# MoBA's position bias: from two TensorE products per head to VectorE, and the two heads' value products interleaved

## The reference, cut to what matters

```
s_own = einsum('bhqd,bhkd->bhqk', q_c, k_own) + rel_bias[:, rel_bucket(q_pos - k_pos)]
s_own = where(k_pos <= q_pos, s_own, -inf)
probs = softmax(s_own)
out   = einsum('bhqk,bhkd->bhqd', probs, v_own)
```

## Time and profile before

| | |
|---|---|
| median of the runs | 2476.46 us (2475.26 to 2477.57) |
| span of the profiled execution | 2475.7 us |
| PE busy | 2411.7 us, 97% |
| PEld busy | 2055.0 us, 83% |
| DVE busy | 1606.0 us, 65% |
| ACT busy | 1033.3 us, 42% |
| mean granted TensorE clock | 0.994 |
| MoBA stage of layer 0 | 302.98 to 327.60 us |
| MoBA stage of layer 1 | 1001.31 to 1025.93 us |

### The profile page before, as it was taken

The page is one execution under the profiler, slowest core; times in us unless marked ns, Lnnn a source line. Parts: engine busy times, 40 slices in busy tenths (PEclk is TensorE's granted clock), DMA queues, the critical chain, the costliest instruction groups (busy, mean ns, idle before and its releaser), DMA issues. The chain is left out here.

```text
span 2475.7 us, 41693 instructions
## 1 busy us (share of the span) xinstructions
PE 2411.7 (97%) x17447; PEld 2055.0 (83%) x17447; DVE 1606.0 (65%) x2242; ACT 1033.3 (42%) x1365; POOL 99.2 (4%) x179
## 2 busy tenths in 40 slices
PE   7999999999999999999999999999999999998999
PEld 7999989999999999899999854464888887647999
DVE  6887756778888887657798632671744442474555
ACT  5445534454554455335454321661422222263333
POOL 2010000001101100000001000000000000000000
PEclk9999999999999999999999999999999999999999
DMA  8776503647777775116467742102532331212452
GB/s 283 251 271 216 168 3 120 205 145 267 252 254 239 272 244 160 46 54 213 162 229 255 272 155 68 52 2 71 167 102 90 98 102 52 81 56 69 162 195 69
DMA packets 270807, 381.97 MB, mean 154 GB/s; under 512 B 9593, under 2 KB 235209, under 8 KB 268994
## 3 DMA queue, kind: packets, MB, share of 16 engines
q1 hardware_dynamic: 251628, 314.47, 38.7%
q0 software_dynamic: 18128, 64.20, 7.2%
q10 hardware_dynamic: 902, 1.15, 0.2%
HBM read 366.13 MB, written 13.65 MB: 153 GB/s over the span
## 5 line engine op out<-in xcount | busy, mean ns | idle before, releaser
L704 PE MATMUL ps<-span 128*128 128x512 f32 x1280 | 453.9, 399 | 2.3 <-issue 1.2
L635 PE MATMUL ps<-span,w_low 128*128 128x256 f32 x1440 | 408.0, 283 | 0.0
L706 PE MATMUL ps<-span,w_low 128*128 128x256 f32 x1280 | 359.5, 281 | 0.0
L633 PE MATMUL ps<-span 128*128 128x256 f32 x1216 | 348.6, 287 | 8.2 <-DVE span L1585 5.2
L1603 DVE TENSOR_TENSOR w_low<-ring,span 128x2048 fp32r<-128x2048 f32 x131 | 299.8, 2288 | 82.3 <-ACT span L1267 82.3
L1267 ACT ACTIVATE span<-ring 128x2048 fp32r<-128x2048 f32 x131 | 250.6, 1915 | 135.5 <-DMA ring<-in_ffn_w_in 112.8
L704 PEld LDWEIGHTS ps<-span 128*128 128x128 f32 x1280 | 240.6, 188 | 60.3 <-issue 1.3
L635 PEld LDWEIGHTS ps<-span,w_low 128*128 128x128 f32 x1440 | 277.0, 192 | 0.0
L634 PE MATMUL ps<-span 128*128 128x256 f32 x864 | 245.3, 284 | 0.0
L633 PEld LDWEIGHTS ps<-span 128*128 128x128 f32 x1216 | 233.8, 192 | 12.4 <-DVE w_low L1603 5.4
L706 PEld LDWEIGHTS ps<-span,w_low 128*128 128x128 f32 x1280 | 241.9, 189 | 0.0
(11 more groups left out here) (487 smaller groups left out, 5337.3 us busy)
## 6 DMA issues: line engine op xcount, KB each, us to landing
ring<-in_ffn_w_in SPq DMA_DIRECT2D x88, 1024.0 KB, 8.9
ring<-in_w_mlp SPq DMA_DIRECT2D x64, 1024.0 KB, 5.3
wmod<-in_w_mod POOLq DMA_DIRECT2D x96, 512.0 KB, 6.8
ring<-in_ffn_w_out SPq DMA_DIRECT2D x44, 1024.0 KB, 5.2
ring<-in_w_mix_in SPq DMA_DIRECT2D x26, 1024.0 KB, 5.5
ring<-in_xattn_w_kv SPq DMA_DIRECT2D x16, 1024.0 KB, 5.4
mod_scratch<-mod_acc POOLq DMA_DIRECT2D x24, 512.0 KB, 6.2
ring<-mod_scratch SPq DMA_DIRECT2D x12, 1024.0 KB, 4.9
```

Of the source, the lines that this page charges most:

```text
L633: mm(dst, w_hi, x_hi, start=start, stop=False, **more)
L635: return mm(dst, w_lo, x_hi, start=False, stop=stop, **more)
L704: mm(ps[bank + m].rearrange("p (w t) -> p w t", w=2), hi[:, k, cols], span[:, :, k, :], start=(k == 0), stop=False, skip_group_check=True)
L706: last = mm(ps[bank + m][:, 0:T], lo[:, k, cols], h_high[:, k, :], start=False, stop=(k == KD - 1), skip_group_check=True)
```

## The change: the bias is added by VectorE, and a pair's value products alternate

The table becomes `toep`, with toep[p, h, t] = bias_rows[h, 127 - p + t], so that its rows stand in the order of the queries and nothing has to be reversed. To read it with one DMA of positive strides, GpSimd first stores 128 copies of each row (2 MB where it was 16 KB) and reads with a row stride of 511. The reversing matrix leaves the constants.

TensorE's `scores(h)` keeps the two products of queries and keys alone. For h >= 4 it waits for the two maxima of head h - 4, no longer for the exponentials. VectorE's two row maxima become two `tensor_tensor_reduce`: each adds scores from PSUM and bias from `toep`, writes the sum to `prob` and the row maximum to `smx`. For h >= 4 it waits first for the turn of head h - 4, the last reader of that slot of `prob`. ScalarE takes the exponential in place, from `prob` to `prob`, and the wait for the turn leaves it. The wait for the table moves from TensorE to VectorE.

`out(h)` becomes `out_pair(pair)`: the products of the even and the odd head over the first 128 keys, then the two over the last 128 keys, one after the other. It waits for both heads' `probT`. It stands at even steps h >= 4, between scores(h) and turn(h - 2), and the last pair comes at the end.

```diff
             def scores(h):
                 if h >= 4:
-                    pe.wait_ge(*sm_act.at(l, 2 * (h - 3)))
+                    pe.wait_ge(*sm_max.at(l, 3 * (h - 4) + 2))
-                mm(bank[:, 0:T], cst["flip"], hank[:, h, :], start=True, stop=False,
-                mm(bank[:, T:T + P], cst["flip"], hank[:, h, P:T], start=False, stop=False,
...
+                mm(bank[:, 0:T], mq[hi, pair, P:T], mk[hi, pair, :], start=True, stop=True)
+                mm(bank[:, T:T + P], mq[hi, pair, 0:P], mk[hi, pair, 0:P], start=True, stop=True
+                   ).then_inc(*sc_done.up())
...
+            def out_pair(pair):
+                pe.wait_ge(*pt_ready.at(l, 2 * pair + 2))
+                if pair >= 2:
+                    pe.wait_ge(*av_out.at(l, pair - 1))
+                bank = ps[6 + pair % 2]
+                for k, at, width in ((0, 0, T), (1, P, P)):
+                    for e in range(2):
+                        h = 2 * pair + e
+                        last = mm(bank[e * HD:(e + 1) * HD, at:T], mv[:, k, h * HD:(h + 1) * HD],
+                                  probT[:, e, k * T:k * T + width], start=(k == 0), stop=(k == 1),
+                                  skip_group_check=True)
+                        if k == 1:
+                            last.then_inc(*av_done.up())
...
-            for h in range(NH + 3):
+            for h in range(NH + 2):
                 if h < NH:
                     scores(h)
+                if h >= 4 and h % 2 == 0:
+                    out_pair((h - 4) // 2)
                 if 2 <= h < NH + 2:
                     turn(h - 2)
-                if h >= 3:
-                    out(h - 3)
+            out_pair(NPAIR - 1)
...
-                pool.dma_start(scratch["bias"], bias_rows).then_inc(bias_stored.sem, 16)
+                pool.dma_start(scratch["bias"], bias_rows.rearrange("h (o t) -> h o t", o=1).to_broadcast(
+                    [NH, P, 2 * T])).then_inc(bias_stored.sem, 16)
                 pool.wait_ge(bias_stored.sem, 16)
                 src = scratch["bias"]
-                pool.dma_start(hank[:, :, :], bass.AP(src.tensor, 0, [[1, P], [2 * T, NH], [1, T]])
+                pool.dma_start(toep[:, :, :], bass.AP(src.tensor, P - 1, [[2 * T - 1, P], [P * 2 * T, NH], [1, T]])
                                ).then_inc(bias_stored.sem, 16)
...
             def exponential(h):
-                e, g, bank = h % 4, base + h, ps[banks[h % 4]]
+                e, g = h % 4, base + h
+                bank = prob[:, e, :] if biased else ps[banks[h % 4]]
                 act.wait_ge(*sm_max.at(l, 3 * (g + 1)))
-                if h >= 4:
-                    act.wait_ge(*pt_done.at(l, g - 3))
...
             def maxima(h):
                 e, g = h % 4, base + h
                 dve.wait_ge(*sc_done.at(l, g + 1))
+                if biases and h >= 4:
+                    dve.wait_ge(*pt_done.at(l, g - 3))
...
+                    if biases:
+                        v.tensor_tensor_reduce(prob[:, e, at:at + w], ps[banks[e]][:, at:at + w], biases(h, t), 1.0,
+                                               -3.0e38, ALU.add, ALU.max, smx[:, e, t:t + 1]).then_inc(*sm_max.up())
+                    else:
+                        v.tensor_reduce(smx[:, e, t:t + 1], ps[banks[e]][:, at:at + w], AX_X, ALU.max
+                                        ).then_inc(*sm_max.up())
...
+            if l == 0:
+                dve.wait_ge(bias_stored.sem, 32)
+            maxima, weights = softmax(l, 0, 1.0, (T, P), SCORE_BANKS, lambda h, t: toep[:, h, t * P:T])
```

More of the change, by code:

```diff
@@ L113, in constants @@
         "head_ones": f(r // HD == c // HD),
-        "flip": f(r + c == P - 1),
         "eye": f(j == t),
@@ L270, in program @@
         store["v_loaded"] = [Signal(ctx, nc, f"v_loaded{s}") for s in range(RING2)]
-        scratch = {"bias": nc.dram_tensor("bias_scratch", (NH, 2 * T), F32).ap(),
+        scratch = {"bias": nc.dram_tensor("bias_scratch", (NH, P, 2 * T), F32).ap(),
                    "mod": nc.dram_tensor("mod_scratch", (DEPTH, P, 2, MODS * P), F32).ap()}
@@ L312, in build_first @@
         part("under_mem", [P, KD, T])
-        part("under_hank", [P, NH, T])
+        part("under_toep", [P, NH, T])
         g_low = part("g_low", [P, KD, T])
@@ L335, in build_first @@
     mem_sb = sb("mem_sb", [P, KD, T])
-    hank = sb("hank", [P, NH, T])
+    toep = sb("toep", [P, NH, T])
     mix_buf = sb("mix_buf", [P, RAW + 4 * T])
@@ L789, in scores @@
                 if h >= 4:
-                    pe.wait_ge(*sm_act.at(l, 2 * (h - 3)))
+                    pe.wait_ge(*sm_max.at(l, 3 * (h - 4) + 2))
                 hi = slice(hb, hb + HD)
-                mm(bank[:, 0:T], cst["flip"], hank[:, h, :], start=True, stop=False,
-                   skip_group_check=True)
-                mm(bank[:, T:T + P], cst["flip"], hank[:, h, P:T], start=False, stop=False,
[L796 to L800, removed]
+                mm(bank[:, 0:T], mq[hi, pair, P:T], mk[hi, pair, :], start=True, stop=True)
+                mm(bank[:, T:T + P], mq[hi, pair, 0:P], mk[hi, pair, 0:P], start=True, stop=True
+                   ).then_inc(*sc_done.up())
             def turn(h):
@@ L809, in turn @@
                 last.then_inc(*pt_done.up())
[L811 to L814, removed]
+            def out_pair(pair):
+                pe.wait_ge(*pt_ready.at(l, 2 * pair + 2))
+                if pair >= 2:
                     pe.wait_ge(*av_out.at(l, pair - 1))
[L816 to L820, removed]
+                bank = ps[6 + pair % 2]
[7 more added lines that the diff above has]
+                            last.then_inc(*av_done.up())
             pe.wait_ge(*mix_evac.at(l, MIX_TILES - 1))
-            if l == 0:
-                pe.wait_ge(bias_stored.sem, 32)
-            for h in range(NH + 3):
+            for h in range(NH + 2):
                 if h < NH:
                     scores(h)
+                if h >= 4 and h % 2 == 0:
+                    out_pair((h - 4) // 2)
                 if 2 <= h < NH + 2:
                     turn(h - 2)
-                if h >= 3:
-                    out(h - 3)
+            out_pair(NPAIR - 1)
         def heads_of(e):
@@ L1340, in cross_part, with softmax @@
                ).then_inc(*cross_high.up())
-        def softmax(l, base, scale, widths, banks):
+        def softmax(l, base, scale, widths, banks, biased=False):
             def exponential(h):
-                e, g, bank = h % 4, base + h, ps[banks[h % 4]]
+                e, g = h % 4, base + h
+                bank = prob[:, e, :] if biased else ps[banks[h % 4]]
                 act.wait_ge(*sm_max.at(l, 3 * (g + 1)))
-                if h >= 4:
-                    act.wait_ge(*pt_done.at(l, g - 3))
                 at = 0
@@ L1469, in scalar_program @@
             col_high(l, KV0)
-            exponential, turned = softmax(l, 0, 1.0, (T, P), SCORE_BANKS)
+            exponential, turned = softmax(l, 0, 1.0, (T, P), SCORE_BANKS, True)
             for h in range(NH + 2):
@@ L1751, in shift, with softmax @@
                                                b[:, m, 1:T + 1], ALU.mult, ALU.add), mixed)
-        def softmax(l, base, scale, widths, banks):
+        def softmax(l, base, scale, widths, banks, biases=None):
             def maxima(h):
@@ L1969, in vector_program @@
             step(l, v.memset(state[:, :, :], 0.0), seq_step)
-            maxima, weights = softmax(l, 0, 1.0, (T, P), SCORE_BANKS)
+            if l == 0:
+                dve.wait_ge(bias_stored.sem, 32)
+            maxima, weights = softmax(l, 0, 1.0, (T, P), SCORE_BANKS, lambda h, t: toep[:, h, t * P:T])
             evac = moba_out(l)
```

2 lines of the change are left out of this document (removed).

## The result

The changed kernel is slower: 2497.18 us median of 4 runs (2493.37 to 2503.82), beside 2477.02 of the kernel before on the same chip (2475.26 to 2479.95). The ratio is 1.0088, with an interval of 1.007 to 1.0105. The forecast was 2471.1 us, the range up to 2477.5. Its profiled execution took 2495.78 us with a span of 2493.8, against a span of 2475.7 before: 18.1 us more.

The account below looks back on a forecast made before the run. TensorE's issue was taken to bound the stage before, a cross-engine loop and VectorE after. Gaining 2.7 us in each of two layers, 5.4, takes 2475.7 to 2470.3; plus 0.8 gives 2471.1 us, range 2467 to 2477.5.

Parts of the forecast that it names:

- The edits that I cost at nothing: Table store of 2 MB: some 12 us, up to twice that under load, weight loads still in time; no cost.
- The walk: Layer 0's stage laid out by durations and engine orders: solver starts at 325.56, a gain of 2.67 us.
- anywhere outside the two stages: Sign against the forecast: time moving outside this stage of layer 0 and its twin in layer 1.
- The loop: Stage, across TensorE, VectorE and ScalarE: out_pair waits for ScalarE's copy; 3.95 + M, 4.8 us a pair against 5.96.
- TensorE's terms: TensorE's work per pair in the stage: scores 2 x 0.85, turns 2 x 0.48, value products 0.80, together 3.46 us.
- The stage at full clock: Layer 0's stage after the change, from 302.98 to some 325.1; 22.10 us forecast.
- M: VectorE's time for both row maxima of a head with the new instruction: 0.85 us, between 0.62 and 0.93.
- The first (TensorE stays the limit, 2456.5): Rival in the stage: TensorE stays the limit, gain 10.0 us a layer, 2456.5 us; chance 0.07.
- The second (a slow instruction): Rival on VectorE: new instruction slow, slower from M = 1.26; 2479.9 us at M = 1.50; chance of slower 0.12.
- The third (no overlap of alternated products): Rival on TensorE: alternated products don't overlap with 256 columns, 1.60 us a pair; 2475.8 us, no change; chance 0.04.

Follow-up runs that it names:

- e2: The kernel before with the 2 MB store alone, 128 copies of each row from SBUF; 2493.18 us, ratio 1.0067.
- e10: The kernel before with 16 KB stored once, then copied 128-fold from DRAM to DRAM, heads as outer dimension; 2474.48 us, ratio 0.9995.
- e5: e1 with unread TensorE products filling every gap: 4 behind the scores of head 2, then 2, 3, 4, 1 before the pairs; 2472.96 us.
- e3: e1 with four unread TensorE products behind the scores of head 2; 2478.33 us, ratio 1.0006.
- e8: e1 with ScalarE's copy before the exponential, VectorE's low half at step 9, unread products behind head 2's scores and before pairs 3 and 4; 2466.98 us.
- e11: e8 with only the 3 unread products behind the scores of head 2, none before the pairs; 2462.76 us, ratio 0.995.
- e1: The changed kernel with the 16 KB store again, rows reversed in the table and read backwards by VectorE; 2483.01 us, ratio 1.0026.
- e4: The kernel before with the alternated value products (out_pair) alone, flip products and small store kept; 2482.23 us, ratio 1.0017.
- e9: The kernel before with 16 KB stored once, then copied 128-fold from DRAM to DRAM, copies as outer dimension; 2475.06 us, ratio 0.999.

## Why the prediction was wrong

**The step that failed first** is "The edits that I cost at nothing". It took the 2 MB store from the rate of a load to 128 partitions, 1 MB in 6.0 us, at 12 us and "at up to twice that under load". It took 45.0, with the ring's loads at 37.0, where a delay of "as much as 10 us" was allowed for. The step looked for who waits for the table, and there it was right: the table landed 45 us before VectorE asked for it. What counted were the ring's loads, under way on another queue at the same time. e2 shows this alone at 12.57 us of late start; e10 shows that the source, not the bytes, made it so. The price was in no row of before, and the text bounded it by a row of another kind of source.

**The second failed step** is "The walk". The stage of before stood "at full clock", and the walk took every duration of the new one at that clock, with no term for its loss. The text itself put 1.1 us of idle time ahead of each out_pair, and its walk leaves TensorE with nothing between the third head's scores, done by 302.98 + 3 x 0.85 = 305.53, and the first turn (maxima 2, behind the weights that this turn needs, stand at 306.75). It never asked what a TensorE that is busy 1.5 of 4 us does to its clock. In before the flip products filled this time beside their own job; unread products in their place bring the clock back (e5). The walk's gain of 2.67 us a layer turned into a loss of 4.9 in layer 0 and 3.4 in layer 1 (stage and solver). e5 undoes that by adding work.

**Also wrong was the bound on where the time could move**, "anywhere outside the two stages" would refute it, and it did: 13.19 us ahead of the first, and 3.46 and 1.95 in the solvers, where the lowered clock lasted on in both.

**What held.** The loop: out_pair does wait, 0.92 and 1.21 us at full clock, for ScalarE's copy (e3), and the two changed orders together, ScalarE's copy first and VectorE's low half later, take the stage at full clock from 21.7 (e5) to 18.1 us (e8, which also has 5 added products a layer and not 14). Which of the two orders did it was not separated. TensorE's terms: 0.80 for a pair's products (e3), 3.46 a pair (e11: 3.45). The stage at full clock: 22.10 forecast, 21.71 in e5. M was 0.65 against 0.85: the read-out exists, but the next instruction starts at its start (1020.56 for both), so it adds 0.08 us once and not 0.20. The Trainium skill, "VectorE: DVE Perf Modes", section "Two Vector instructions with no wait between them", says that such an operation is two instructions; the trace agrees that there are two, at a lower price than the prediction took for the second. By the prediction's own 5.5 us a layer for each us of M, that would have given 1.1 more; the stage gave 0.4, so 0.7 is missing; whether e5's own added products or a term of the loop took it is open.

**The rivals.** The first (TensorE stays the limit, 2456.5) falls by e3's waits, and comes half true only with the orders changed (e11). The second (a slow instruction) falls by M = 0.65. The third (no overlap of alternated products) falls by 0.80 us. The right answer, slower, stood in the second alone: it had its 0.12 for a reason that did not happen.

**Still open.** What exactly lowers the clock. It fell after TensorE had been busy 1.59 of 4 us (after), 1.54 of 4 (e1) and 3.17 of 5 (e3); yet at the end of e11's stage it was busy 2.09 of 4 us and the clock stayed at 1.00:
```profile
313.00:318.00 5.00, 4.23 (x32) 2.73 (x30) 4.17 (x22) 3.82 (x15) 0.00 (x0) 1.00 0.00 0
318.00:322.00 4.00, 2.09 (x17) 1.58 (x18) 3.15 (x4) 0.92 (x2) 0.00 (x0) 1.00 0.00 0
```
The runs of one kernel lie up to 14 us apart (e8), and time goes with their mean clock (e4, e11 above). The traces show where. ScalarE rounds the same weight tile at 1361.7 us in e8 and at 1360.9 in e11, and a later one at 1652.1 and 1645.7. In between, in the second block, e8's granted clock is 0.96, 0.91 and 0.96 in the three stretches of 40 us from 1400 to 1520, and e11's is 1.00. From 1440 to 1480 TensorE is busy 36.70 us in both, with the same program. The same holds for e10 beside e9 (1373.7 and 1372.8 before, 1663.1 and 1657.5 behind). Why the clock falls there in one execution and not in the next is open. It limits what the medians can tell to some 3 to 5 us. The two stages are measured better by the time at which layer 1's recurrence begins, 1050.26 us in before: e5 stands at 1044.32, 5.9 us earlier where the forecast had 5.4, e8 and e11 11.9 and 11.7 earlier, e4 3.6 later, e1 10.0 later, the changed kernel 21.2 later.

## What to carry to other kernels

When work is taken from the engine that is the limit, list its idle times after the change and look at the granted clock of the stretches that already have such gaps; a gap there may cost more than the work did, and some idle work in it pays (e5, e11). A DMA of many bytes from few partitions is to be priced by its source and by who else has transfers under way, not by its reader's deadline. Where a loop over three engines becomes the bound, look at the order on the engine in its middle: here that, with one unrelated instruction moved on VectorE, was worth 3.6 us a stage (e5 to e8).

## What the runs showed of the hardware

- 2 MB from 8 SBUF partitions to DRAM took 45.0 us (DMA share 0.50 from 236 to 256 us), and multiplied the landing time of other loads by seven (5.3 to 37.0); from DRAM in the same shape it took 16.0, with the copies outermost 10.5.
- `tensor_tensor_reduce` from PSUM and SBUF takes 0.42 us for 256 columns and 0.29 for 128 (e1), plus a read-out of 0.08 that overlaps the next instruction; reading the table backwards (e1) changes nothing:
```profile
304.42 0.42 DVE L1757 CUSTOM_DVE_ANT_0 prob<-ps,toep 128x256 f32<-128x256 f32 x1 [3.53 <-PE ps L793]
304.77 0.08 DVE L1757 DVE_READ_ACCUMULATOR2_ANT smx<- 128x1 f32 x1
304.77 0.29 DVE L1757 CUSTOM_DVE_ANT_0 prob<-ps,toep 128x128 f32<-128x128 f32 x1
```
- Once at half clock, TensorE stayed there through 20 us in which it was busy 3.0 to 5.0 of every 5 us, and came back in the solver's dense stretch (165 records in 5 us, 345 to 350 us).
- Almost the same stretch of program can run at either clock: from 1440 to 1480 us TensorE is busy 36.70 us in e8 at a granted clock of 0.91, and 36.70 us in e11 at 1.00.
